# Hybrid streaming encoder on one core: the attention stage unrolled over head pairs, small and large query tiles in turn, and the softmax factor applied to the output

## What is computed

```python
logits = jnp.einsum('bthd,btkhd->bthk', q, k_sel) * (HEAD_DIM ** -0.5)
logits = jnp.where(valid[:, :, None, :], logits, -jnp.inf)
probs = jax.nn.softmax(logits, axis=-1)
out = jnp.einsum('bthk,btkhd->bthd', probs, v_sel)
```

## Time and profile before

| what | value |
|---|---|
| median of 3 executions | 1770.56 us (1768.44 to 1771.08) |
| the profiled execution: its time / its span | 1767.36 us / 1765.7 us |
| mean granted clock of PE over the span | 0.975 of 2.4 GHz |
| busy shares over the span: PE, DVE, ACT, POOL | 92%, 53%, 37%, 28% |
| attend_heads, first logits matmul to last output copy | 453.8 to 665.7 us |

### The profile page before, as it was taken

The page is one execution under the profiler, slowest core; times in us unless marked ns, Lnnn a source line. Parts: engine busy times, 40 slices in busy tenths (PEclk is TensorE's granted clock), DMA queues, the critical chain, the costliest instruction groups (busy, mean ns, idle before and its releaser), DMA issues. The chain is left out here.

```text
span 1765.7 us, 23638 instructions
## 1 busy us (share of the span) xinstructions
PE 1623.6 (92%) x8451; PEld 1395.7 (79%) x8451; DVE 939.1 (53%) x1501; ACT 644.6 (37%) x1322; POOL 487.8 (28%) x335
## 2 busy tenths in 40 slices
PE   5988999999687788999899999999999999999995
PEld 5975999877455556879777989888888889888884
DVE  6338999895665565530855333343443333434438
ACT  6346577943566564322633211111111111111112
POOL 5133112147633423212113322121212221121116
PEclk9999999999789999999999999999999999999999
DMA  5122211111100004313233211111011111111006
GB/s 196 57 66 64 82 47 38 58 63 40 31 28 27 2 25 147 126 50 106 84 120 105 63 49 36 48 36 48 26 46 48 48 48 36 48 36 48 25 23 179
DMA packets 88189, 108.16 MB, mean 61 GB/s; under 512 B 6080, under 2 KB 65216, under 8 KB 88128
## 3 DMA queue, kind: packets, MB, share of 16 engines
q1 hardware_dynamic: 88128, 107.35, 20.0%
HBM read 88.05 MB, written 19.28 MB: 61 GB/s over the span
## 5 line engine op out<-in xcount | busy, mean ns | idle before, releaser
L155 POOL TENSOR_TENSOR w_lo_ring<-w_raw_ring,w_hi_ring 128x1024 fp32r<-128x1024 f32 (+1 forms) x97 | 237.6, 2461 | 815.4 <-ACT w_hi_ring L149 814.9
L1959 DVE TENSOR_TENSOR f_y<-f_y,ps 128x512 f32<-128x512 f32 (+1 forms) x288 | 195.7, 685 | 257.6 <-PE ps L200 257.6
L186 PE MATMUL ps<-hth,w_hi_ring 128*128 128x384 f32 (+2 forms) x1176 | 267.8, 331 | 4.2 <-PEq L1643 1.8
L186 PE MATMUL ps<-htl,w_hi_ring 128*128 128x384 f32 (+2 forms) x1176 | 266.3, 330 | 0.0
L186 PE MATMUL ps<-hth,w_lo_ring 128*128 128x384 f32 (+2 forms) x1176 | 266.3, 330 | 0.0
L200 PE MATMUL ps<-w_hi_ring,f_fh 128*128 128x512 f32 (+1 forms) x576 | 226.8, 394 | 18.8 <-DVE f_y L1959 18.8
L200 PE MATMUL ps<-w_hi_ring,f_fl 128*128 128x512 f32 (+1 forms) x576 | 224.7, 390 | 0.0
L200 PE MATMUL ps<-w_lo_ring,f_fh 128*128 128x512 f32 (+1 forms) x576 | 224.6, 390 | 0.0
L186 PEld LDWEIGHTS ps<-hth,w_hi_ring 128*128 128x128 f32 (+1 forms) x1176 | 203.6, 189 | 8.2 <-issue 5.4
L186 PEld LDWEIGHTS ps<-hth,w_lo_ring 128*128 128x128 f32 (+1 forms) x1176 | 202.8, 188 | 0.6
L186 PEld LDWEIGHTS ps<-htl,w_hi_ring 128*128 128x128 f32 (+1 forms) x1176 | 202.8, 188 | 0.6
(11 more groups left out here) (240 smaller groups left out, 2640.2 us busy)
## 6 DMA issues: line engine op xcount, KB each, us to landing
w_raw_ring<-in_w SPq DMA_DIRECT2D x64, 512.0 KB, 3.8
w_raw_ring<-in_w_in SPq DMA_DIRECT2D x24, 512.0 KB, 3.8
n_xin<-in_x_prompt SPq DMA_DIRECT2D x8, 512.0 KB, 5.8
w_raw_ring<-in_w_o SPq DMA_DIRECT2D x8, 512.0 KB, 4.0
oe_x<-in_x_prompt SPq DMA_DIRECT2D x8, 512.0 KB, 4.3
x<-oe_new SPq DMA_DIRECT2D x8, 512.0 KB, 5.0
me_x<-x SPq DMA_DIRECT2D x8, 512.0 KB, 4.1
x<-me_new SPq DMA_DIRECT2D x8, 512.0 KB, 5.0
```

The lines of the kernel that those rows point to most:

```text
L155: pool.tensor_tensor(self.lo[:, slot, 0:width], self.raw[:, g % 2, 0:width], self.hi[:, slot, 0:width].bitcast(F32), ALU.subtract).then_in ...
L186: last = pe.matmul(c.ps[0:width, bank + b, 0:size], part[:, slot, k * width:(k + 1) * width], x[:, k, o:o + size], start=(k == 0 and n == ...
L1959: dve.tensor_tensor(out, out, ps[0:r, u % 2, :], ALU.add).then_inc(y_added, 1)
```

## The change

attend_heads is rewritten:

- The loop over pairs is gone; all 72 units are written out in one list for each engine, and steps run on from one head and pair to the next. The base of the semaphores and its increments go; V has two buffers.
- Within a head the order of the tiles is 0, 7, 1, 6, 2, 5, 3, 4, sample.
- DVE's add of the mask takes logits and mask with the factor -1/8 and a row minimum, and its accumulator is what exp takes as its bias. The instruction at L1276 goes.
- The probabilities are not scaled (L1285 goes). The row sums of a head are kept; one reciprocal for four tiles is taken (three in a head). PE transposes each column of reciprocals, broadcast to 128 columns, into a block (9 small transposes for each head, `sums`); ACT copies such a block to SBUF (h_rsum), and DVE multiplies the product with it on its way to the output (`leave`). That takes the place of ACT's copy at L1203 and L1205.
- For tiles 4 to 7, the first group of four transposed blocks is copied by DVE, not ACT.
- h_pt holds each tile's blocks at their own place; a product reads two tiles with a stride. Products of the second head of a pair go to partitions 64 to 127. The sample's product goes to bank 6 and waits until the first half of that head's output has left it.
- PE's list for step g is: logits of g, transposes of g-2, product of g-3 where due, sums of g-4 where due. ACT's high parts are at steps 1, 2 and 3 of a pair.

The core of the diff:

```diff
-    pt = m.put("h_pt", [P, NP, SEQ])
+    vs = m.put("h_v", [P, 2, NP + 3, P])
+    pt = m.put("h_pt", [P, MOFF[NP]])
+    rsum = m.put("h_rsum", [P, 512])
+    ORDER = [0, 7, 1, 6, 2, 5, 3, 4, NP]
+    EVENT = {2: 0, 3: 3, 6: 1, 7: 2, 8: NP // 2}
+    LEAVE = {6: 0, 7: 1, 8: 2}
+    def on_dve(i, n):
+        return NP // 2 <= i < NP and n == 0
...
# ScalarE
-            with act.Fori(0, NG) as p:
+            def sums(g):
+                act.wait_ge(tr_done, q + 1)
+                if e:
+                    act.wait_ge(pv_out, e)
+                act.activation(rsum[rows, 0:n], ps[rows, 4 + q % 2, 0:n], ACT.Copy).then_inc(rsum_done, 1)
+            for g in range(UNITS + 5):
+                if g >= 5 and (g - 5) % NT in LEAVE:
+                    sums(g - 5)
...
+                if 0 <= g - 2 < UNITS:
+                    copies(g - 2)
+                if g < UNITS:
...
+                    act.activation(s, s, ACT.Exp, scale=-1.0, bias=low[0:r, g % 3:g % 3 + 1], accum_out=su[0:r, hh, i:i + 1]).then_inc(exp_done, 1)
# VectorE
-                        dve.tensor_scalar(nm[0:r, j:j + 1], mx[0:r, j:j + 1], -(HD ** -0.5), None, ALU.mult).then_inc(nm_done.sem, 1)
-                        dve.tensor_scalar(s, s, rc[0:r, j:j + 1], None, ALU.mult).then_inc(scaled.sem, 1)
+            def leave(g):
+                dve.wait_ge(pv_done, len(EVENTS) * hd + EVENTS.index(x) + 1)
+                dve.wait_ge(rsum_done, 3 * hd + part + 1)
+                dve.tensor_tensor(c.cat[rows, p, 512 * part:512 * part + n], ps[rows, 6 + part % 2, 0:n], rsum[rows, 0:n], ALU.mult).then_inc(pv_out, 1)
+            for g in range(UNITS + 5):
...
+                if 0 <= g - 2 < UNITS:
+                    copies(g - 2)
+                if 0 <= g - 3 < UNITS and (g - 3) % NT in LEAVE:
+                    reciprocals(g - 3)
+                if g >= 5 and (g - 5) % NT in LEAVE:
+                    leave(g - 5)
# TensorE
+            def sums(g):
+                pe.wait_ge(rc_done, 3 * hd + part + 1)
+                empty(q)
+                for x, t in enumerate(range(*tiles_of(part).indices(NT))):
+                    last = pe.transpose(ps[:, 4 + q % 2, x * P:x * P + r], rc[0:r, hh, t:t + 1].broadcast_to([r, P]), c.ident[0:r, 0:r])
+                last.then_inc(tr_done, 1)
...
+                if q == NP // 2:
+                    pe.wait_ge(pv_out, 3 * hd + 1)
...
+            for g in range(UNITS + 4):
+                if g < UNITS:
+                    logits(g)
+                if 0 <= g - 2 < UNITS:
+                    transposes(g - 2)
+                if 0 <= g - 3 < UNITS and (g - 3) % NT in EVENT:
+                    output(g - 3)
+                if g >= 4 and (g - 4) % NT in LEAVE:
+                    sums(g - 4)
```

More of the change, by code:

```diff
@@ L1134, in attend_heads @@
+    assert m.at <= stacks.at
     m.at = stacks.end
     sm = m.put("h_s", [P, 3, SEQ])
[L1136 to L1157, removed]
@@ new lines, in emptied, with copies_end, groups_end, tiles_of @@
+    def emptied(q):
+        return sum(emptied_by(x) == emptied_by(q) for x in range(q + 1))
+    def copies_end(g, who):
+        return sum(emptied_by(x) == who for x in range(groups_end(g)))
+    def groups_end(g):
+        return first_group[g] + len(blocks_of(unit(g)[3]))
+    def tiles_of(part):
+        return slice(4 * part, min(4 * part + 4, NT))
+    def pv_before(g):
+        hd, p, hh, i = unit(g)
+        q = NP // 2 if i == NP else i // 2
+        return len(EVENTS) * (hd - 1) + EVENTS.index(max(x for x in EVENT if EVENT[x] == q)) + 1
@@ L1180, in _, with copies @@
         @block.scalar
         def _(act):
[L1182 to L1188, removed]
+            def copies(g):
+                hd, p, hh, i = unit(g)
+                if pv_before(g) > 0:
+                    act.wait_ge(pv_done, pv_before(g))
+                for n, blocks in enumerate(blocks_of(i)):
+                    if on_dve(i, n):
+                        continue
+                    q = first_group[g] + n
@@ L1207, in _ @@
[L1207 to L1229 removed]
+                        act.activation(pts[0:DEC, 2, :], ps[0:DEC, b, 2 * DEC:3 * DEC], ACT.Copy).then_inc(act_copied, 1)
@@ L1299, in transposes @@
+            def transposes(g):
+                hd, p, hh, i = unit(g)
+                r = rows_of(i)
+                pe.wait_ge(exp_done, g + 1)
+                for n, blocks in enumerate(blocks_of(i)):
+                    q = first_group[g] + n
+                    empty(q)
                     for x, j in enumerate(blocks):
                         k = min(P, LIM[i] - j * P)
-                        last = pe.transpose(ps[0:k, 4 + q % 2, x * r:(x + 1) * r], sm[0:r, u % 3, j * P:j * P + k], c.ident[0:r, 0:r])
@@ new lines, in output @@
+                    if hd and q in (0, 3):
+                        pe.wait_ge(pv_out, 3 * (hd - 1) + (3 if q == 0 else 2))
+                    a = 2 * q
+                    step = a + 1
+                    tiles = pt[:].rearrange("p (b n) -> p b n", n=P)
+                    for j in range(a + 2):
+                        o = 256 * (q % 2)
+                        if j <= a:
+                            at = MOFF[a] // P + j
+                            moving = tiles[:, at:at + step + 1:step, :]
+                            out = ps[rows, 6 + q // 2, o:o + 256].rearrange("p (t n) -> p t n", t=2)
+                        else:
+                            moving = pt[:, MOFF[a + 1] + j * P:MOFF[a + 1] + j * P + P]
+                            out = ps[rows, 6 + q // 2, o + P:o + 256]
+                        last = pe.matmul(out, v[:, j, :], moving, start=(j == 0), stop=(j == a + 1))
```

251 lines of the change are left out of this document (130 added, 121 removed).

## The result

The changed kernel took 1756.15 us (median of four executions, 1754.96 to 1759.04) beside 1770.82 for the kernel before on the same chip: ratio 0.9922, interval 0.9904 to 0.9939. It is faster, as forecast, and inside the range, but by 14.7 us and not by 27.6. The profiled execution took 1755.51 us.

The account below looks back on a forecast made before the run. A round through PE, DVE, ACT and back bounds the stage, not one engine. 17.8 us PE work plus 4.2 to 4.5 waits: 22.3 a head, gain 27.6, 1739.8 us profiled, 1743 median; range 1720 to 1759 (8 in 10).

Parts of the forecast that it names:

- The three waits: PE's waits in each head: 0.95 us for large transposes, 1.6 for the sample's product, 1.3 for the last small transpose.
- the list of steps: Hand-made layout of one head over four engines' lists: 17.8 us PE work plus 4.2 to 4.5, 22.3 us.
- POOL in time: POOL's low parts for a pair's second head ready at 20.5 us, needed at 22.3; its chain ends at 38 of 44.6.
- the four rivals: PE packed (0.18), POOL's chain setting the pair (0.07), longer waits of the same kind (0.08), slower clock (0.05).
- the first step: PE's work in attention: 16.9 us a head plus 0.9 for nine added small transposes, 17.8 us.
- waits and clock: What the forecast called the other 20 us of a 53.7 us pass, beyond 33.8 us of priced PE work.
- position 6: Step in a head's tile order whose product is largest, 3.2 us; first one forecast to start at about 465 us.
- the tail: End of the attention stage, from seven further heads done at 621 us to the last multiplication at 638: 17 us.
- the second step: Stages behind attention were to be only shifted, not changed, so the stage's 27.6 us gain would reach the total.
- Nearly 9 us each at three seams, 26: Between passes over head pairs: 3.7 us PE idle plus some 5 of half-clock ramp per seam, saved by one list.
- No scaling: Dropping L1285 takes its length (mean 819 ns) and its stretching beside POOL out of the round through the engines.
- that unseen load of the prediction: Stationary operand of one broadcast column in the sums' transposes, absent from the trace; priced as a normal transpose, 0.9 us a head.

Follow-up runs that it names:

- e7: Changed kernel with a DVE pass over the probabilities (times 1.0, in place) put back between exp and transposes: 1790.16 us, ratio 1.0104 to before.
- e12: Changed kernel with two unread ACT copies (1.2 us) added ahead of the output projection: 1756.25 us, ratio 0.9912 to before.
- e15: Kernel before with four unread ACT copies (2.3 us) added ahead of the output projection: 1777.37 us, ratio 1.0023 to before unedited.
- e10: Changed kernel with 20 and 32 filler transposes in PE's waits around the start of the output projection: 1758.51 us, ratio 0.9923 to before.
- e13: Changed kernel with four unread ACT copies (2.3 us) added ahead of the output projection: 1752.38 us, ratio 0.9891 to before.
- e2: Changed kernel with the sample's product in a free logits bank, without its wait for the leaving output: 1747.32 us, ratio 0.9854 to before.
- e4: Changed kernel, but each pair of heads finishes all products and sums before the next pair's first logits: 1774.14 us, ratio 1.0011 to before.
- e9: Kernel before without the scaling instruction L1285 and the reciprocals, so no division by row sums: 1752.71 us, ratio 0.9895 to before unedited.
- e6: Changed kernel without normalising: no reciprocals, transposes of sums, their copies or the product with them: 1742.66 us, ratio 0.9847 to before.

## Why the prediction was right and wrong

**Right: direction, and the form of the new stage.** The three waits came where the list of steps had them: 0.68 us for the large transposes (0.95 forecast), 1.30 for the sample's product (1.6), 1.01 for the small transpose (1.3), and 0.1. Three waits a head that no row of before showed were read from the order of four lists. Clock 1.00 from 462 to 643 us, DVE's copies at 687 ns (685 forecast), POOL in time: as said. None of the four rivals came. The rule of the Trainium skill's SBUF — State Buffer (Who interferes with whom) that I weighed agrees with the traces on both sides: e7's SBUF to SBUF pass was stretched, 1.95 to 2.32 us for 384 columns beside POOL against 0.35 without, and after's copies from PSUM were not.

**Wrong, the first step: "16.9 + 0.9 = 17.8 us a head".** It measured 20.5. The prices inside a group were right (17.7 by those of after); what was missing is the borders: about 0.3 us at each product of V, less elsewhere, 2.1 us a head, and 0.65 at the ends before the waits. This could have been read from the kernel before. There too a product that I priced at 1.5 us stands from 545.33 to 546.99, 1.66, between logits and transposes:

```profile
545.33 1.73 PE L1323 MATMUL ps<-h_pt,h_v 128*64 128x256 f32 x8
546.99 0.77 PE L1301 MATMUL ps<-ident,h_s 128*128 128x128 f32 x5
```

I did not use it, since I booked all that was not streaming under "waits and clock". The waits were smaller than forecast, 3.1 for 4.2 to 4.5, and hid part of the error; a PE that has more to do arrives later where it waits, which may be why, but no run shows it. That the time still lies in the range is owed to the range's width. So a head has 23.5 us and not 22.3. The first position 6 came earlier (463.4, forecast 465), seven heads end at 627.9 (621), the tail has 18.6 us (17), and the stage ends at 646.5 and not 638: 8.5 of the missing us.

**Wrong, the second step: "Stages after it are shifted and not changed".** In the profiled executions they took 6.9 us more, the rest of what is missing. e12 to e15 show that this is not work of the new attention: two or four idle copies move the part between 1098.7 and 1106.7 us in after and between 1099.1 and 1105.0 in before. What changes is which of PE's later waits is followed by a stretch at half clock. e10 shows that the clock with which the part begins is not it. But the traces don't make it chance from one execution to the next either. All eight traces with after's order, sums and no added copies pay it, the three of before's kind don't, and no execution of after is as fast as e13's two; in e2, on the other hand, single executions differ by 7.6 us, as if it changed there from one to the next. The kernel after as it stands seems to pay these 7 us, by when its waits fall; what decides between the two outcomes of one wait, and why after falls on this side, stays open. By medians, which include it, the change is worth 14 to 15 us; by the stages alone 16.4 or 20.7, by which execution of before is taken.

**Wrong, the parts of the gain.** "Nearly 9 us each at three seams, 26" is a term that was mis-sized: e4 measured 5.6 each, 16.8, in the new order (the sum that gave 27.6 does not use it). I had counted PE's idle time and the whole ramp as gain; that PE waits 3.1 us a head in the unbroken list too may be the difference, but no run takes the two apart. The step *No scaling* had the right mechanism, and e9 gives its size: 17 to 21 us in the old loop. What I priced too low is its substitute. I took 0.9 us of PE a head and parts of the waits; e6 gives 14.8 us of the stage, 1.85 a head. Measured against what scaling cost the old loop, most of the saving on L1285 went into that.

So where did the large change go? Leaving out the seams is worth 17 us. Leaving out the scaling is worth 17 to 21 in the old loop, of which 14.8 would be spent on the blocks; put back into the new order it costs 30.7. The parts do not add up to the whole, and only their sum, 16 to 21 us of the stage, is measured for the change as it is. The alternation's 9 us were spent on the sample's wait, 7.5; e2 wins that back. That wait (1.6 us a head by the forecast) was in my list before the run, with its cause. I used it as a cost, and did not ask whether the product needed that bank; in the kernel before it had another.

## What to carry to other kernels

Price PE's work from stretches with the same mixture of kinds as the new program will have: in a list of short pieces the borders between kinds cost 2 us of a 23 us head here, most of it at the products. When an instruction moves, ask which bank it had and why: the sample's product lost 7.5 us by a new one. When an instruction is replaced, measure both forms against leaving it out, in the same loop: the new form of the factor cost 14.8 us in the new loop (e6), the old one 17 to 21 in the old (e9), and 31 put back into the new (e7). And when a change only shifts later stages of a throttled engine, allow several us either way for them: repeats of both kernels with a dummy delay of 1 and 2 us tell how much of a difference is only timing.

## What the runs showed of the hardware

- The same eight transposes behind the same wait of 2.02 us of PE took 1.48 to 1.94 us in nine traces and 1.06 to 1.13 in ten, wholly or partly at half clock in the nine. Over the 1100 us behind the stage 10 to 37 us were at half clock, by trace, and the time went roughly with it: 1099.8 us with 10 (before), 1106.7 with 31 (after).
- Adding 2.3 us of work made one kernel's profiled execution 3.7 us faster (e13 against after) and the other kernel slower by 5.5 us in the median (e15).
- Behind another kind of work the first logits matmul of 512 columns took 0.34 us to the next start where the following ones took 0.23 to 0.24. Behind transposes this is nearly made up for, since the last transpose is followed after 0.03 us instead of 0.11; around a product of V nothing makes up for it, and its two borders cost about 0.3 us.
- One DVE operation from SBUF to SBUF on 384 columns (L1340 in e7) took 0.35 us four times and 1.95 to 2.32 beside POOL's work four times; DVE's copies of 512 columns from PSUM took 0.69 us with and without POOL.
- Transposes whose stationary operand is one column broadcast (L1374) cost what normal ones do, 0.109 us to the next start and 0.41 for four: that unseen load of the prediction was priced rightly.
